# FFN gate and up products of a transformer kernel in another order: pairs of 512-column matmuls, then pairs of 256-column ones

## The chip, the cores and the metric

The kernel runs on one core of a Trainium2 chip. The metric is the device time of one execution in microseconds; the time before is the median of three runs.

## The reference, cut to what matters

Two blocks of two layers each work on 256 tokens with 1024 features. Every layer has two feed-forward networks (FFN), with 2816 hidden features, around its mixers, so eight FFNs are computed in all. The reference in fp32:

```python
D_MODEL, SEQ, DEPTH, D_FF = 1024, 256, 2, 2816

def swiglu(x, w_gate, w_up, w_down):
    return (jax.nn.silu(x @ w_gate) * (x @ w_up)) @ w_down

def first_block(x, ...):
    for l in range(DEPTH):
        x = layer_norm(ALPHA * x + 0.5 * swiglu(x, ffn1_w_gate[l], ffn1_w_up[l], ffn1_w_down[l]), ...)
        ...
        x = layer_norm(ALPHA * x + 0.5 * swiglu(x, ffn2_w_gate[l], ffn2_w_up[l], ffn2_w_down[l]), ...)
    return x
```

The second block has the same form of FFN, with gate and up weights in one matrix. The change touches `x @ w_gate` and `x @ w_up` alone.

## The kernel before

All weights come in pieces of 128x1024 fp32 values (512 KB) through one DMA queue into a ring of six buffers. ScalarE rounds a piece to fp32r, the type of the matmul operands, as `w_hi` (L717); VectorE (in some stages GpSimd) computes the rest, `w_lo = raw - w_hi` (L943). Activations are split likewise; `in_both` holds for each of KD = 8 row tiles k the 256 tokens of the high part and, next to them, the 256 of the low part, and `in_hi` is its first half. A product of full precision is then hi x hi + hi x lo + lo x hi.

For most linear layers the three are three matmuls of 256 columns (`three`, L391 to L393, also used by `begin` for the first gate and up piece of an FFN). For the down product of an FFN and some other outputs they are three matmuls of 512 columns (`three_rows`, L407 to L409).

The gate and up products of the hidden tiles 1 to 21 (`gate_up`) take another form. A piece is the 1024x128 slice of the gate (i = 0) or up (i = 1) weights for a tile of 128 hidden features, as eight row tiles of 128x128. For each row tile k there is one 512-column matmul (L517) with the high weights on both parts of the activations, which goes to the left and right halves of a PSUM bank, and one 256-column matmul (L519) with the low weights on the high part of the activations, which is added to the left half. Each matmul has its own weight load of 128x128 before it. The last matmul of the piece signals `piece_used`; behind that signal ScalarE takes the right half out (L759, `part`) and VectorE adds the left half (L1039), and the split buffer of the piece can be filled again. The engine's program order sets the order of matmuls; for a tile j it is gate piece, up piece, then the down product of tile j - 1 (four banks, twelve matmuls of 512 columns). A gate or up piece begins with a wait for `split_low`, and a down product with waits for its piece and for the hidden values.

Eight FFNs x 21 tiles x 2 pieces x 8 row tiles make 2688 executions of L517 and of L519.

Of the kernel before, what the change touches and what calls it, by code (L numbers as in the profile page):

```python
# [25 lines left out]
S = 256  # L26
LAYERS = 2
KD = D // P
# [116 lines left out]
def build(nc, a, out, stop=None):  # L145
    ctx = ExitStack()
    with ctx:
        def sb(name, shape, dt=F32):
            return ctx.enter_context(nc.sbuf_tensor(name, shape, dt))
# [3 lines left out]
        def sem(name):  # L153

            if name not in sems:
                sems[name] = ctx.enter_context(nc.semaphore(name))
            return sems[name]
# [14 lines left out]
        in_both = sb("in_both", [P, KD, 2, S], F32R)  # L172
        in_hi, in_lo = (in_both[:, :, i, :] for i in range(2))
# [214 lines left out]
        def three(o, left, right, first, last, **kw):  # L388

            (lh, ll), (rh, rl) = left, right  # L390
            nc.tensor.matmul(o, lh, rh, start=first, stop=False, **kw)  # L391
            nc.tensor.matmul(o, lh, rl, start=False, stop=False, **kw)  # L392
            return nc.tensor.matmul(o, ll, rh, start=False, stop=last, **kw)  # L393

        def piece(e, k=KD):

            return [w[:, e % SPLIT, :].rearrange("p (k c) -> p k c", k=k) for w in (w_hi, w_lo)]

        def at2(pair, *index):
            return [v[index] for v in pair]  # L400

        def three_rows(b, e, left_hi, left_lo, first, last, **kw):

            t, d = divmod(b, 2)
            o, tok, cols = ps[:, b, :], slice(t * P, (t + 1) * P), slice(d * 512, (d + 1) * 512)
            right_hi, right_lo = w_hi[:, e % SPLIT, cols], w_lo[:, e % SPLIT, cols]
            nc.tensor.matmul(o, left_hi[:, tok], right_hi, start=first, stop=False, **kw)  # L407
            nc.tensor.matmul(o, left_hi[:, tok], right_lo, start=False, stop=False, **kw)  # L408
            return nc.tensor.matmul(o, left_lo[:, tok], right_hi, start=False, stop=last, **kw)  # L409
# [66 lines left out]
        def gate_up_bank(j, i):  # L476

            return ps[:, 4 + 2 * (j % 2) + i, :]
# [9 lines left out]
        def pe_ffn(pe, n, e0, chunk, seeds=None, fold=None):  # L488


            def begin():


                for c in range(KD // 2):

                    pe.wait_ge(sem("in_ready"), chunk + c + 1)
                    for i in range(TOGETHER):
                        if c == 0:

                            pe.wait_ge(sem("split_low"), e0 + i + 1)  # L500
                        w = piece(e0 + i)
                        for k in (2 * c, 2 * c + 1):
                            mm = three(ps[:, FIRST_BANK, i * S:(i + 1) * S], at2(w, ALL, k, ALL),
                                       at2(given, ALL, k, ALL), k == 0 and i == 0, k == KD - 1, skip_group_check=True)
                        if c == KD // 2 - 1:
                            mm.then_inc(sem("piece_used"), 1)

            def gate_up(j, it=0):
                for i in range(2):
                    e = e0 + 3 * j - 1 + i  # L510

                    pe.wait_ge(sem("split_low"), e + 1 + it * RAW)
                    hi, lo = piece(e)
                    bank = gate_up_bank(j, i)
                    for k in range(KD):

                        nc.tensor.matmul(bank.rearrange("p (a t) -> p a t", a=2), hi[:, k, :], in_both[:, k, :, :], start=(k == 0),  # L517
                                         stop=False, skip_group_check=True)
                        mm = nc.tensor.matmul(bank[:, 0:S], lo[:, k, :], in_hi[:, k, :], start=False, stop=(k == KD - 1),  # L519
                                              skip_group_check=True)  # L520
                    mm.then_inc(sem("piece_used"), 1)

            def down(j, it=0, last=False):
                e = e0 + (FFN_PIECES - 1 if last else 3 * j + 4)
                pe.wait_ge(sem("split_low"), e + 1 + it * RAW)

                pe.wait_ge(sem("hidden_ready"), (ffn0 + n) * TILES + j + 1 + it * 2)
                for b in range(4):
                    if seeds is not None and j == 0 and b % 2 == 0:

                        pe.wait_ge(sem("seeded"), HALF * seeds + b // 2 + 1)
                    mm = three_rows(b, e, hid_hi[:, j % 2, :], hid_lo[:, j % 2, :], j == 0 and seeds is None, last,
                                    skip_group_check=seeds is not None)
                    if last and b < 3:

                        mm.then_inc(sem("rows_out"), 1)
                mm.then_inc(sem("piece_used"), 1)

            def spread():

                pe.wait_ge(sem("diag_ready"), fold + 1)
                for t in range(HALF):
                    mm = nc.tensor.matmul(ps[:, SPREAD_BANK, t * P:(t + 1) * P], ones[:, 0:P], diag[:, t, :], start=(t == 0),
                                          stop=(t == HALF - 1), skip_group_check=True)
                mm.then_inc(sem("spread_ready"), 1)

            begin()
            if fold is not None:
                spread()
            gate_up(1)  # L550
            down(0)
            with pe.Fori(0, TILES // 2 - 1) as it:
                for j in (2, 3):
                    gate_up(j, it)
                    down(j - 1, it)
            down(TILES - 1, last=True)
# [2126 lines left out]
```

## Time and profile before

| | us |
|---|---|
| runs: median (lowest to highest of three) | 2742.33 (2737.32 to 2743.27) |
| profiled execution: span from first to last instruction | 2732.5 |
| TensorE matmuls busy | 2683.6 |
| TensorE weight loads busy (beside the matmuls) | 2350.2 |
| VectorE busy | 1840.9 |
| ScalarE busy | 1401.1 |
| GpSimd busy | 217.3 |

The profile gives the execution by its span alone. Busy time is the time covered by instructions of an engine. Matmuls are pipelined: one starts long before the one ahead of it has ended, so that the rate of TensorE is read from the distances between starts in the timeline, and not from durations. Weight loads overlap the matmul that runs.

### The profile page before, as it was taken

Reading aid. Unit: us, or ns where it says so; the run is one execution under the profiler, and the core shown is the slowest. Engines: PE = TensorE matmul, PEld = TensorE weight load, DVE = VectorE, ACT = ScalarE, POOL = GpSimd, SP = SyncE. Lnnn points to the kernel's source line nnn. Section 1 sums busy time; section 2 is a strip of 40 time slices with the busy share of each in tenths; the row PEclk is TensorE's granted clock in tenths of the full one; section 3 lists DMA queues with packets and bytes.
Section 4 is the critical chain, followed back from the end, with each engine's and each line's share of the span. In section 5 each row is a group of like instructions: output and inputs, shape, how many; then the busy total and the mean of one; then the engine's idle time right before and its main releaser. Section 6 shows DMA issues by size and latency. Waiting matters only on the chain.

```text
span 2732.5 us, 47833 instructions
## 1 busy us (share of the span) xinstructions
PE 2683.6 (98%) x18836; PEld 2350.2 (86%) x18836; DVE 1840.9 (67%) x2891; ACT 1401.1 (51%) x2191; POOL 217.3 (8%) x95
## 2 busy tenths in 40 slices
PE   9999999999999999999999999999999999999999
PEld 7889788888978888889898898888888899998887
DVE  6667766766867677767732856777775863475777
ACT  5455544544564454456623556445446652455544
POOL 0000000000000000005225000000003422400000
PEclk9999999999999999999999999999999999999999
DMA  8765366577535656663413554665674421564564
GB/s 254 216 183 176 105 189 189 174 220 199 167 122 174 188 157 201 187 190 113 116 57 117 174 181 132 196 188 177 185 213 128 123 86 56 162 194 133 177 190 131
DMA packets 623403, 445.38 MB, mean 163 GB/s; under 512 B 28096, under 2 KB 589536, under 8 KB 622880
## 3 DMA queue, kind: packets, MB, share of 16 engines
q1 hardware_dynamic: 623264, 443.43, 54.6%
q8 instruction: 99, 1.62, 0.2%
q14 instruction: 40, 0.33, 0.0%
HBM read 442.32 MB, written 1.05 MB: 162 GB/s over the span
## 4 chain that ended last, share of the span: by engine, by line
PE 89%; DVE 8%; ACT 1%; issue 1%; DMA 0%; POOL 0%; DVEq 0%; SPq 0%; ACTq 0%
PE ps L517 23%; PE ps L519 11%; PE ps L391 8%; PE ps L392 8%; PE ps L393 8%; PE ps L407 7%; PE ps L408 7%; PE ps L409 7%; DVE w_lo L943 2%; PE ps L702 1%; PE ps L678 1%; PE ps L1708 1%; PE ps L1698 1%; PE ps L1670 1%; DVE moments L1111 1%
## 5 line engine op out<-in xcount | busy, mean ns | idle before, releaser
L943 DVE TENSOR_TENSOR w_lo<-raw,w_hi 128x1024 fp32r<-128x1024 f32 x704 | 860.4, 1224 | 418.9 <-ACT w_hi L717 418.1
L717 ACT ACTIVATE w_hi<-raw 128x1024 fp32r<-128x1024 f32 x800 | 844.7, 1056 | 478.6 <-PE ps L409 240.1
L517 PE MATMUL ps<-in_both,w_hi 128*128 128x512 f32 x2688 | 956.4, 398 | 1.7 <-DVE w_lo L943 1.7
L519 PE MATMUL ps<-in_both,w_lo 128*128 128x256 f32 x2688 | 754.1, 281 | 0.0
L517 PEld LDWEIGHTS ps<-in_both,w_hi 128*128 128x128 f32 x2688 | 505.0, 188 | 126.7 <-DVE w_lo L943 4.0
L519 PEld LDWEIGHTS ps<-in_both,w_lo 128*128 128x128 f32 x2688 | 507.5, 189 | 6.1
L391 PE MATMUL ps<-in_both,w_hi 128*128 128x256 f32 x1664 | 486.1, 292 | 23.6 <-DVE in_both L1020 8.3
L392 PE MATMUL ps<-in_both,w_hi 128*128 128x256 f32 x1664 | 471.9, 284 | 0.0
L393 PE MATMUL ps<-in_both,w_lo 128*128 128x256 f32 x1664 | 471.7, 283 | 0.0
L759 ACT ACTIVATE work<-ps 128x256 f32<-128x256 f32 x336 | 129.5, 385 | 538.0 <-PE ps L519 538.0
L943 POOL TENSOR_TENSOR w_lo<-raw,w_hi 128x1024 fp32r<-128x1024 f32 x90 | 216.8, 2413 | 2136.7 <-ACT w_hi L717 2136.7
L391 PEld LDWEIGHTS ps<-in_both,w_hi 128*128 128x128 f32 x1664 | 319.5, 192 | 38.5 <-issue 11.9
L392 PEld LDWEIGHTS ps<-in_both,w_hi 128*128 128x128 f32 x1664 | 319.7, 192 | 1.0 <-issue 0.5
L393 PEld LDWEIGHTS ps<-in_both,w_lo 128*128 128x128 f32 x1664 | 319.7, 192 | 0.0
L407 PE MATMUL ps<-w_hi,hid_hi 128*128 128x512 f32 x704 | 276.9, 393 | 2.4 <-DVE ps L1149 2.4
L408 PE MATMUL ps<-w_lo,hid_hi 128*128 128x512 f32 x704 | 275.9, 392 | 0.0
L409 PE MATMUL ps<-w_hi,hid_lo 128*128 128x512 f32 x704 | 274.1, 389 | 0.0
L1039 DVE TENSOR_TENSOR work<-ps,work 128x256 f32<-128x256 f32 x336 | 141.8, 422 | 105.2 <-ACT work L759 102.7
L407 PEld LDWEIGHTS ps<-w_hi,hid_hi 128*128 128x128 f32 x704 | 132.1, 188 | 36.8 <-DVE ps L1149 3.7
L409 PEld LDWEIGHTS ps<-w_hi,hid_lo 128*128 128x128 f32 x704 | 132.2, 188 | 29.2
L408 PEld LDWEIGHTS ps<-w_lo,hid_hi 128*128 128x128 f32 x704 | 132.2, 188 | 21.0
L991 DVE TENSOR_TENSOR in_both<-arena,in_both 128x512 fp32r<-128x512 f32 x44 | 31.6, 744 | 89.1 <-ACT in_both L723 88.9
(348 smaller groups left out, 3019.7 us busy)
## 6 DMA issues: line engine op xcount, KB each, us to landing
raw<-in_w_ffn_in SPq DMA_DIRECT2D x176, 512.0 KB, 3.7
raw<-in_w_mix SPq DMA_DIRECT2D x112, 512.0 KB, 3.7
raw<-in_ffn_w_gate SPq DMA_DIRECT2D x88, 512.0 KB, 3.8
raw<-in_ffn_w_up SPq DMA_DIRECT2D x88, 512.0 KB, 3.7
raw<-in_ffn_w_down SPq DMA_DIRECT2D x88, 512.0 KB, 3.8
raw<-in_w_ffn_out SPq DMA_DIRECT2D x88, 512.0 KB, 4.0
raw<-in_w_in SPq DMA_DIRECT2D x40, 512.0 KB, 3.8
raw<-in_w_out SPq DMA_DIRECT2D x32, 512.0 KB, 3.5
```

Of the source, the lines that this page charges most:

```text
L391: nc.tensor.matmul(o, lh, rh, start=first, stop=False, **kw)
L392: nc.tensor.matmul(o, lh, rl, start=False, stop=False, **kw)
L393: return nc.tensor.matmul(o, ll, rh, start=False, stop=last, **kw)
L407: nc.tensor.matmul(o, left_hi[:, tok], right_hi, start=first, stop=False, **kw)
L408: nc.tensor.matmul(o, left_hi[:, tok], right_lo, start=False, stop=False, **kw)
L409: return nc.tensor.matmul(o, left_lo[:, tok], right_hi, start=False, stop=last, **kw)
L517: nc.tensor.matmul(bank.rearrange("p (a t) -> p a t", a=2), hi[:, k, :], in_both[:, k, :, :], start=(k == 0), stop=False, skip_group_check ...
L519: mm = nc.tensor.matmul(bank[:, 0:S], lo[:, k, :], in_hi[:, k, :], start=False, stop=(k == KD - 1), skip_group_check=True)
L717: nc.scalar.activation(w_hi[:, e % SPLIT, :], raw[:, e % RAW, :], ACT.Copy).then_inc(sem("split_high"), 1)
L759: nc.scalar.activation(part[:, j % 2, i, :], gate_up_bank(j, i)[:, S:2 * S], ACT.Copy)\
L943: eng.tensor_tensor(w_lo[:, e % SPLIT, :], raw[:, e % RAW, :], w_hi[:, e % SPLIT, :].bitcast(F32), ALU.subtract)\
L1039: nc.vector.tensor_tensor(o, gate_up_bank(j, i)[:, 0:S], part[:, j % 2, i, :], ALU.add).then_inc(sem("summed"), 1)
```

## The change

In `gate_up`, the loop over the eight row tiles becomes a loop over four pairs of neighbouring row tiles. Within a pair the two 512-column matmuls are issued first, and then the two 256-column ones. The same sixteen matmuls with the same operands go to the same bank; the first (k = 0) still starts the accumulation, the last (k = 7, low weights) still ends it and signals the piece. Nothing else is changed.

```diff
-                    for k in range(KD):
-
-                        nc.tensor.matmul(bank.rearrange("p (a t) -> p a t", a=2), hi[:, k, :], in_both[:, k, :, :], start=(k == 0),
-                                         stop=False, skip_group_check=True)
-                        mm = nc.tensor.matmul(bank[:, 0:S], lo[:, k, :], in_hi[:, k, :], start=False, stop=(k == KD - 1),
-                                              skip_group_check=True)
+                    for c in range(KD // 2):
+                        for k in (2 * c, 2 * c + 1):
+
+                            nc.tensor.matmul(bank.rearrange("p (a t) -> p a t", a=2), hi[:, k, :], in_both[:, k, :, :],
+                                             start=(k == 0), stop=False, skip_group_check=True)
+                        for k in (2 * c, 2 * c + 1):
+                            mm = nc.tensor.matmul(bank[:, 0:S], lo[:, k, :], in_hi[:, k, :], start=False, stop=(k == KD - 1),
+                                                  skip_group_check=True)
                     mm.then_inc(sem("piece_used"), 1)
```

## Rows read from the trace of the kernel before

**Rows 1.** The page: busy time, the granted clock in 40 slices, the chain by engine.
```profile
PE 2683.6 (98%) x18836; PEld 2350.2 (86%) x18836; DVE 1840.9 (67%) x2891; ACT 1401.1 (51%) x2191; POOL 217.3 (8%) x95
...
PEclk9999999999999999999999999999999999999999
...
PE 89%; DVE 8%; ACT 1%; issue 1%; DMA 0%; POOL 0%; DVEq 0%; SPq 0%; ACTq 0%
```

**Rows 2.** The page's costliest groups: busy us, mean ns, idle before and its releaser.
```profile
L517 PE MATMUL ps<-in_both,w_hi 128*128 128x512 f32 x2688 | 956.4, 398 | 1.7 <-DVE w_lo L943 1.7
L519 PE MATMUL ps<-in_both,w_lo 128*128 128x256 f32 x2688 | 754.1, 281 | 0.0
```

**Rows 3.** The views of line 517 and line 519: durations in ns, least/median/most.
```profile
L517 PE MATMUL ps<-in_both,w_hi x2688: 389/398/501, 21.0 to 2719.7; 128*128 128x512 f32 x192
...
L519 PE MATMUL ps<-in_both,w_lo x2688: 274/281/284, 21.3 to 2719.9; 128*128 128x256 f32 x192
```

**Rows 4.** Timeline of TensorE, a gate and an up piece: start us, duration us, instruction.
```profile
98.11 0.40 PE L517 MATMUL ps<-in_both,w_hi 128*128 128x512 f32 x1
98.34 0.28 PE L519 MATMUL ps<-in_both,w_lo 128*128 128x256 f32 x1
98.46 0.40 PE L517 MATMUL ps<-in_both,w_hi 128*128 128x512 f32 x1
98.69 0.28 PE L519 MATMUL ps<-in_both,w_lo 128*128 128x256 f32 x1
98.81 0.40 PE L517 MATMUL ps<-in_both,w_hi 128*128 128x512 f32 x1
99.05 0.28 PE L519 MATMUL ps<-in_both,w_lo 128*128 128x256 f32 x1
99.17 0.40 PE L517 MATMUL ps<-in_both,w_hi 128*128 128x512 f32 x1
...
102.35 0.40 PE L517 MATMUL ps<-in_both,w_hi 128*128 128x512 f32 x1
```

**Rows 5.** The same timeline: the last product of the up piece, then the down product.
```profile
102.58 0.28 PE L519 MATMUL ps<-in_both,w_lo 128*128 128x256 f32 x1
102.70 0.40 PE L407 MATMUL ps<-w_hi,hid_hi 128*128 128x512 f32 x1
102.93 0.40 PE L408 MATMUL ps<-w_lo,hid_hi 128*128 128x512 f32 x1
103.17 0.39 PE L409 MATMUL ps<-w_hi,hid_lo 128*128 128x512 f32 x1
...
104.08 0.39 PE L407 MATMUL ps<-w_hi,hid_hi 128*128 128x512 f32 x1
...
105.44 0.39 PE L517 MATMUL ps<-in_both,w_hi 128*128 128x512 f32 x1
```

**Rows 6.** Timeline of TensorE where 512-column products turn into a run of 256-column ones.
```profile
1564.06 0.39 PE L409 MATMUL ps<-w_hi,in_both 128*128 128x512 f32 x1
1564.29 0.28 PE L391 MATMUL ps<-in_both,w_hi 128*128 128x256 f32 x1
1564.40 0.28 PE L392 MATMUL ps<-in_both,w_hi 128*128 128x256 f32 x1
1564.52 0.28 PE L393 MATMUL ps<-in_both,w_lo 128*128 128x256 f32 x1
...
1565.84 0.28 PE L392 MATMUL ps<-in_both,w_hi 128*128 128x256 f32 x1
```

**Rows 7.** Timeline of TensorE where the first FFN's 256-column products end.
```profile
20.92 0.28 PE L393 MATMUL ps<-in_both,w_lo 128*128 128x256 f32 x1
21.04 0.40 PE L517 MATMUL ps<-in_both,w_hi 128*128 128x512 f32 x1
21.28 0.28 PE L519 MATMUL ps<-in_both,w_lo 128*128 128x256 f32 x1
```

**Rows 8.** Busy us (instructions) by engine in one stretch: span, PE, PEld, DVE, ACT, POOL.
```profile
60.00:200.00 140.00, 140.00 (x733) 119.26 (x732) 93.19 (x136) 68.74 (x102) 0.00 (x0) 1.00 0.74 205
```

## Prediction

> **What bounds the kernel now.** I read the page first: TensorE's matmuls are busy for 98% of the span, the granted clock is at its full level in all 40 slices, and the chain that ended last is 89% TensorE [rows 1]. So one nanosecond less on each matmul is one less in the total, and one on any other engine is nothing. The costliest groups come next. L517 and L519, the two lines that the change reorders, hold 956.4 and 754.1 us of the busy time, in 2688 products each, with idle time before L517 of only 1.7 us and before L519 of 0.0 [rows 2]. These stages are then neither waiting for pieces nor for drained banks; what is to be read in them is the distance from one matmul's start to the next. The durations don't give that distance (they overlap), but they tell whether a product was held up: the least duration of L517 is 389 ns and its median 398; L519 has 274 and 281 [rows 3]. The usual product in this loop is about 9 ns (512 columns) or 7 ns (256 columns) longer than the least of its kind.
>
> The distances come from the timeline, whose starts are rounded to 10 ns. I call a 512-column product A and a 256-column product B; "A's distance" is from its start to the next start. In the alternating loop, A takes 0.23, 0.23, 0.24 and B 0.12, 0.12, 0.12, a pattern that repeats in 1.06 us; over twelve pairs, 98.11 to 102.35, it is 4.24 us, so 353.3 ns for a pair [rows 4]. In a long run of A alone the distance is 1.36 us / 6 = 226.7 ns (104.08 to 105.44) [rows 5]. In a long run of B alone it is 1.32 us / 11 = 120.0 ns (1564.52 to 1565.84) [rows 6]. An A and a B from uniform runs would make 346.7 ns; the alternating pair costs 6.7 ns more. That excess, 2688 x 6.7 ns = 18 us, is all that an order can touch if the uniform distances are a floor.
>
> **The change part by part.** No product, operand, column or weight load is added or removed: 2688 A and 2688 B before and after, each with its own load. What moves is the order, from A B A B to A A B B in groups of four; there are 2688 / 2 = 1344 groups. Before, a group costs 2 x 353.3 = 706.7 ns.
>
> The trace of before never shows A A B B in a loop, so I put a group together from the nearest transitions:
> - Two A directly behind a B: at the end of a gate or up piece the last B (102.58) is followed by the down product's A at 102.70, 102.93 and 103.17. The two distances make 0.47 us, against 0.453 for two in a uniform run [rows 5]. The four after these take 0.91 us (103.17 to 104.08), which is 0.227 each, so what a B leaves behind is mostly paid by the first two A [rows 5]. Where A follows a uniform run of B (21.04 to 21.28) the first distance reads 0.24 [rows 7], the same within the rounding.
> - Two B directly behind A: the one place where a run of A turns into a run of B has 1564.29, 1564.40, 1564.52, so 0.23 us for two, against 0.240 in the uniform run [rows 6]. The first B is the quick one (0.11).
>
> The sum of a group: 0.47 + 0.23 = 0.70 us. Each term is good to about 10 ns, which is more than the gain in question, so I choose: 701 ns, because the excess over the uniform 693.3 is then 8 ns for the one change from B back to A in a group, near the 6.7 ns that each such change costs in the alternating loop [rows 4]. The gain is 706.7 - 701 = 5.7 ns a group, and 1344 x 5.7 ns = 7.7 us. The bounds: from below the uniform distances, 2 x 226.7 + 2 x 120.0 = 693.3 ns, a gain of 13.3 ns a group and 18 us [rows 5, 6]; from above the longest single distances that these rows show, 0.24 twice and 0.12 twice, 0.72 us, a loss of 13.3 ns a group and again 18 us, 2760 us [rows 4, 7]; it needs the latest A at both places, and no row has two of 0.24 in a row.
>
> The rest comes to nothing. The last instruction of a piece was a B and is a B, and it carries the same signal, so the engines that wait for a piece are told at the same place; the first A of a piece waits as before. The supply of pieces is covered: in the stretch of 60 to 200 us, all of it gate, up and down, VectorE is busy 93.19 of 140.00 us and ScalarE 68.74, with PE at 140.00 [rows 8]. A piece's gain of 23 ns (four groups) in some 2.8 us is far below the third of that time in which VectorE is idle. The down products start behind B B in place of A B; the transition is the same B to A, and I cost it at nothing.
>
> A rule that speaks against any gain: rows 4 to 6 show that a mixed pair isn't the sum of its uniform distances. The Trainium skill (TensorE: Matmul & The Clock Gate, Back-to-back issue gap) gives the isolated distance as columns over 2.4 GHz plus 2.5 ns, a sum in which the order of products has no part; by it a group costs the same in either order and the time stays. The trace disagrees with its size (120.0 ns for 256 columns is over it) and, by the 6.7 ns, with its being independent of the order.
>
> The result: the median of the three runs is 2742.33 us, the profiled span 2732.5; the 9.8 us between lie outside the first and last instruction or in the spread of runs (2737.32 to 2743.27), and the change doesn't touch them. 2742.3 - 7.7 = 2734.6, so 2735 us. Changes under 0.2% (5.5 us) can't be told from none by measuring this kernel; the forecast is just beyond that.
>
> **The rivals.**
> 1. *The excess belongs to each B, or to nothing that order moves.* The load for the product behind a B has only 0.12 us in which to come in, whatever that product is; if the 6.7 ns are owed for each B wherever it stands, two B owe 13.3 ns and the group stays at 706.7. For it: the first A products of rows 5 show that what a B leaves is paid later, not dropped (0.47 for two). Against it: the uniform run of B owes nothing beyond 120.0 [rows 6]. Time 2742; with what lies between, 2739 to 2744.
> 2. *The excess is gone entirely.* If holding up comes only from A and B taking strict turns, the group costs 693.3 ns and the time is 2742.3 - 18 = 2724 us. For it: both uniform runs are clean [rows 5, 6]. Against: the first two A behind a B are together 17 ns over uniform [rows 5], which the quick first B, 10 ns, doesn't pay back in full.
> 3. *The other side: the hold-ups add.* Two short distances ahead of the A A leave the loads of both late; the two A together cost 0.475, between the 0.47 seen and 0.24 twice, and no B is quick (0.12 each). The place is the pair A A behind B B; the price is 715 - 706.7 = 8.3 ns a group, 1344 x 8.3 ns = 11 us, so 2753 us. It decides as soon as two A directly behind two B cost over 467 ns with B at 120 each. For it: [rows 5] has 0.24 for the second A. Against: [rows 6] has a quick B directly behind A.
>
> That the change doesn't do what it says is no rival here: the order of matmuls on one queue is the program's order.
>
> **How the numbers follow.** The forecast, a group of 699 to 704 ns and 2732 to 2739 us, 0.50. Rival 1, 0.22. Rival 2, 0.13. Rival 3, 0.15. Faster by over 0.2% (below 2736.8): three quarters of the forecast's chance, 0.37, and rival 2, together 0.50. Within 0.2%: the rest of the forecast, 0.13, and nearly all of rival 1, 0.20, together 0.33. Slower by over 0.2%: rival 3 and a little of rival 1, 0.17. The range has to hold most of rival 2 (2724) and a part of rival 3, whose size grows from 0 upward to 2753: 2723 to 2750 us.
>
> **What would show it.** Right: in the timeline of the gate and up stage the starts read about 0.23, 0.24, 0.11 or 0.12, 0.12, a piece of sixteen products takes some 23 ns less than before, and a piece's four groups 2.80 us against 2.83. The median duration of the 512-column line falls from 398 towards 393 ns. Rival 1 shows the same sum of four (0.707) with another split. Rival 2 shows medians at the least durations, 389 for A. Rival 3 shows 0.24 twice and medians of 400 or more. The prediction would be wrong if any idle time before these lines rose above the present 1.7 us by several us, or if the clock row left its level.

## The result, and the profile after

The changed kernel takes 2724.81 us (median of six runs, 2721.28 to 2727.11) against 2742.22 us before (six runs, 2734.24 to 2743.27): a ratio of 0.9946, with a 95% interval of 0.9936 to 0.9956. That is 17.4 us less, or 0.54%. The forecast was 7.7 us less and a time of 2735 us. The direction and the range (2723 to 2750) held; the gain is more than twice the one forecast, and lies beside rival 2 (2724 us) rather than the forecast.

The page of the changed kernel: busy time, the granted clock, the chain by engine, and the two groups that were reordered (now L518 and L521).

```profile
PE 2675.0 (98%) x18836; PEld 2351.4 (86%) x18836; DVE 1835.8 (67%) x2891; ACT 1399.7 (51%) x2191; POOL 216.5 (8%) x95
...
PEclk9999999999999999999999999999999999999999
...
PE 90%; DVE 7%; ACT 1%; issue 1%; DMA 0%; POOL 0%; DVEq 0%; SPq 0%; ACTq 0%
...
L518 PE MATMUL ps<-in_both,w_hi 128*128 128x512 f32 x2688 | 843.6, 395 | 1.9 <-DVE w_lo L945 1.9
...
L521 PE MATMUL ps<-in_both,w_lo 128*128 128x256 f32 x2688 | 528.1, 278 | 0.0
```

Nothing has taken TensorE's place: it is still busy for 98%, and the idle time ahead of the reordered line is 1.9 us, where [rows 2] had 1.7. The busy sums (843.6 and 528.1 us against 956.4 and 754.1) are no measure of the gain, as products that follow one of their own line overlap within a group and are counted once. The mean durations are: 395 ns against 398, and 278 against 281.

The timeline of TensorE around the same tile (start us, duration us, instruction; x2 is two products in a row). It answers to [rows 4] and [rows 5].

```profile
98.05 0.62 PE L518 MATMUL ps<-in_both,w_hi 128*128 128x512 f32 x2
98.52 0.40 PE L521 MATMUL ps<-in_both,w_lo 128*128 128x256 f32 x2
98.75 0.63 PE L518 MATMUL ps<-in_both,w_hi 128*128 128x512 f32 x2
99.22 0.39 PE L521 MATMUL ps<-in_both,w_lo 128*128 128x256 f32 x2
99.45 0.63 PE L518 MATMUL ps<-in_both,w_hi 128*128 128x512 f32 x2
...
102.23 0.40 PE L407 MATMUL ps<-w_hi,hid_hi 128*128 128x512 f32 x1
102.47 0.39 PE L408 MATMUL ps<-w_lo,hid_hi 128*128 128x512 f32 x1
102.70 0.39 PE L409 MATMUL ps<-w_hi,hid_lo 128*128 128x512 f32 x1
102.92 0.39 PE L407 MATMUL ps<-w_hi,hid_hi 128*128 128x512 f32 x1
...
104.96 0.62 PE L518 MATMUL ps<-in_both,w_hi 128*128 128x512 f32 x2
```

From 98.05 to 102.23 there are six groups A A B B: 4.18 us, or 697 ns a group, where two alternating pairs took 706.7 ns. The down product takes 2.73 us (102.23 to 104.96); before it took 2.74 (102.70 to 105.44) [rows 5].

Ten nanoseconds of rounding are coarse for this, so from here on I also give distances (from one product's start to the next start) as medians over the 168 tiles of the FFNs, from the trace's starts in whole nanoseconds. Settled distances are those that repeat once the first products of a piece are past. "Gate" is the piece that stands behind a down product, "up" the one that stands behind the gate piece, "down" the twelve products behind both.

| order in a piece | settled distances, ns | gate | up | down | tile |
|---|---|---|---|---|---|
| A B (before) | 241 120 236 113 233 117 | 2810 | 2830 | 2747 | 8387 |
| A A B B (the change) | 233 236 116 113, 233 231 113 119 | 2777 | 2787 | 2730 | 8294 |

The difference is 93 ns a tile, and 168 x 93 ns = 15.6 us: 12.8 us in gate and up, and 2.9 us in the down products, which the change doesn't touch.

The two profiled spans, 2732.5 and 2725.3 us, differ by only 7.2 us. The missing part is the clock. The view of cores of before, of after, and one stretch of after by engine with the granted clock in the third column from the end:

```profile
core 0: 2732.5 us, clock 0.998
```

```profile
core 0: 2725.3 us, clock 0.995
```

```profile
1310.00:1320.00 10.00, 10.00 (x84) 8.94 (x84) 9.04 (x27) 6.31 (x11) 0.00 (x0) 0.83 0.48 139
```

In a few short stretches, one of them inside this row, the clock is at its lower level (1.2 GHz) although PE counts as busy. The page's clock row, in tenths, doesn't show them; the mean of the core does. The stretch itself, and two of its products:

```profile
1315.20:1318.20 3.00, 3.00 (x14) 3.00 (x15) 2.89 (x7) 0.99 (x2) 0.00 (x0) 0.50 1.05 300
```

```profile
1315.50 0.41 PE L392 MATMUL ps<-w_lo,in_both 128*128 128x256 f32 x1
1315.71 0.41 PE L393 MATMUL ps<-w_hi,in_both 128*128 128x256 f32 x1
```

At this level a 256-column product takes 0.21 us from start to start (213 ns) in place of 120. By the traces' clock records, the clock is low for 6.8 us of before and 23.9 us of after with matmuls running, always in stages other than the gate and up products of tiles 1 to 21; it is low too in the last 1.9 and 4.0 us, where no matmul runs. At 213 ns against 120, 44% of the time at the low level is lost, 3.0 and 10.5 us; if it were half, 3.4 and 11.9 us. Without these, the spans are 2729.5 and 2714.8 us, or 2729.1 and 2713.4: 14.7 to 15.7 us apart, beside the 15.6 us of the tiles. The profiled execution of before was simply one with few such stretches.

### The profile page after: what moved, and what is told of

Read it like the earlier page. It is cut to its first block, busy times and chain, and to the rows that moved or that the text cites. A ratio compares the mean times of both kernels' runs of the same rounds, so it can differ in the third digit from the quotient of the medians.

```text
span 2725.3 us, 47833 instructions
## 1 busy us (share of the span) xinstructions
PE 2675.0 (98%) x18836; PEld 2351.4 (86%) x18836; DVE 1835.8 (67%) x2891; ACT 1399.7 (51%) x2191; POOL 216.5 (8%) x95
## 4 chain that ended last, share of the span: by engine, by line
PE 90%; DVE 7%; ACT 1%; issue 1%; DMA 0%; POOL 0%; DVEq 0%; SPq 0%; ACTq 0%
PE ps L518 22%; PE ps L521 11%; PE ps L391 9%; PE ps L392 8%; PE ps L393 8%; PE ps L407 7%; PE ps L408 7%; PE ps L409 7%; DVE w_lo L945 1%; PE ps L704 1%; PE ps L680 1%; PE ps L1710 1%; PE ps L1700 1%; PE ps L1672 1%; DVE moments L1113 1%
## 5 line engine op out<-in xcount | busy, mean ns | idle before, releaser
L518 PE MATMUL ps<-in_both,w_hi 128*128 128x512 f32 x2688 | 843.6, 395 | 1.9 <-DVE w_lo L945 1.9
L521 PEld LDWEIGHTS ps<-in_both,w_lo 128*128 128x128 f32 x2688 | 504.9, 188 | 117.7
L521 PE MATMUL ps<-in_both,w_lo 128*128 128x256 f32 x2688 | 528.1, 278 | 0.0
L393 PE MATMUL ps<-in_both,w_lo 128*128 128x256 f32 x1664 | 474.5, 285 | 0.0
L518 PEld LDWEIGHTS ps<-in_both,w_hi 128*128 128x128 f32 x2688 | 421.0, 189 | 16.0 <-DVE w_lo L945 3.8
L391 PEld LDWEIGHTS ps<-in_both,w_hi 128*128 128x128 f32 x1664 | 322.6, 194 | 38.7 <-issue 11.7
L392 PEld LDWEIGHTS ps<-in_both,w_hi 128*128 128x128 f32 x1664 | 322.9, 194 | 1.0 <-issue 0.5
```

## The experiments

A is a 512-column product, B a 256-column one, as in the prediction. All kernels are the one before with another body of `gate_up`. Those with halved weights leave out part of the result, and those with 384 columns add something to it that doesn't belong there. These six and the one with the right half of the bank ran once each, so they are read by their distances; their times, in us, follow the tiles to within what the clock makes:

| kernel | time, and before beside it | difference | 168 x difference of a tile |
|---|---|---|---|
| A B, 384 columns | 2879.04, 2738.98 | +140.1 | +141.0 |
| A B, A's weights halved | 2706.55, 2738.98 | -32.4 | -31.4 |
| A B, B's weights halved | 2731.69, 2738.98 | -7.3 | -7.9 |
| A B, right half of the bank | 2737.28, 2738.98 | -1.7 | 0 |
| A B, both halved | 2715.84, 2739.79 | -24.0 | -26.9 |
| A A B B, A's weights halved | 2724.54, 2739.79 | -15.3 | -14.6 |
| A A B B, 384 columns | 2888.29, 2739.79 | +148.5 | +158.9 |

**Longer groups.** The change again, four and four, and eight and eight, all on one chip.

```diff
-                    for c in range(KD // 2):
-                        for k in (2 * c, 2 * c + 1):        # A
-                        for k in (2 * c, 2 * c + 1):        # B
+                    for c in range(KD // n):                # n = 4: quads, n = 8: octs
+                        for k in range(n * c, n * c + n):   # A
+                        for k in range(n * c, n * c + n):   # B
```

> The change itself, beside the two longer groupings. Both theories: 2723 to 2728 us; sixteen products of a piece take 2777 to 2790 ns from start to start in the timeline (before: 2810 to 2830).

> Four 512-column products (A), then their four 256-column ones (B). Theory 'turn': each turn from B back to A costs a fixed few ns over the uniform distances (226.7 for A, 120 for B); the change has one turn in four products and an excess of 3.7 ns over 693.3 there, so one turn in eight halves it: 695.2 ns for four products, a piece of 2781 ns on average, some 2.5 us less in all than the change. Theory 'load': the weight load that runs beside a B is late by about 7 ns wherever B stands; then only the number of B counts, and a piece stays at 2782 to 2790 ns, the time within 1 us of the change.

> All eight A of a piece, then its eight B. Theory 'turn': one turn in sixteen products, a piece at 2773.3 plus about 4 ns = 2777 ns, some 3 to 4 us less than the change. Theory 'load': B distances settle at 120 and A at 226.7, a piece at 2780 to 2790 ns, the time within 1 us of the change.

Measured against 2741.36 us before (eleven runs): the change 2725.15 us, ratio 0.9944 (0.9932 to 0.9956); four and four 2727.24 us, 0.9955 (0.9942 to 0.9967); eight and eight 2723.16 us, 0.9938 (0.9926 to 0.9950). The intervals overlap; the distances are sharper. 'Gate', 'up', 'down' and 'tile' are in ns.

| order in a piece | settled distances, ns | gate | up | down | tile |
|---|---|---|---|---|---|
| A A B B | 233 236 116 113, 233 231 113 119 | 2777 | 2787 | 2730 | 8294 |
| 4 A, 4 B | 235 233 236 224 117 120 120 120, 233 236 228 232 118 119 118 117 | 2780 | 2807 | 2767 | 8354 |
| 8 A, 8 B | 233 236 228 233 231 227 227 227, 113 119 120 ... 120 | 2766 | 2793 | 2748 | 8307 |

The timeline of the kernel with four and four (its up piece and the first product behind it):

```profile
98.41 1.09 PE L517 MATMUL ps<-in_both,w_hi 128*128 128x512 f32 x4
99.33 0.64 PE L519 MATMUL ps<-in_both,w_lo 128*128 128x256 f32 x4
99.81 1.09 PE L517 MATMUL ps<-in_both,w_hi 128*128 128x512 f32 x4
100.74 0.63 PE L519 MATMUL ps<-in_both,w_lo 128*128 128x256 f32 x4
101.21 0.40 PE L407 MATMUL ps<-w_hi,hid_hi 128*128 128x512 f32 x1
```

The timeline of the kernel with eight and eight:

```profile
97.66 1.98 PE L517 MATMUL ps<-in_both,w_hi 128*128 128x512 f32 x8
99.47 1.11 PE L519 MATMUL ps<-in_both,w_lo 128*128 128x256 f32 x8
100.43 2.00 PE L517 MATMUL ps<-in_both,w_hi 128*128 128x512 f32 x8
102.27 1.11 PE L519 MATMUL ps<-in_both,w_lo 128*128 128x256 f32 x8
103.22 0.40 PE L407 MATMUL ps<-w_hi,hid_hi 128*128 128x512 f32 x1
```

The first eight A, behind a down product, take 1.81 us, 226.7 ns each by whole nanoseconds; the second eight, behind eight B, take 1.84 (100.43 to 102.27). The some 27 ns between them are what the first five A pay (233 236 228 233 231). So neither theory holds: the cost of a turn from B to A isn't a fixed few ns (it is 3.7 ns over uniform distances in A A B B, and about 20 in eight and eight), and it isn't the same per B either (four and four is worse than both its neighbours). The forecast of a further 2.5 us for four and four was wrong in sign: by distances it gives back 168 x 60 ns = 10 us. Its median hides this, since its six runs had mean clocks of 0.998 to 1.000, and the before runs beside them 0.993 to 0.998; its profiled execution spans 2724.4 us at a clock of 1.000, with matmuls never at the low level, against 2713.4 to 2714.8 for the change with its low stretches taken off.

**A longer second product.** Alternating, with 384 columns in place of 256.

```diff
-                        mm = nc.tensor.matmul(bank[:, 0:S], lo[:, k, :], in_hi[:, k, :], ...)
+                        mm = nc.tensor.matmul(bank[:, 0:384], lo[:, k, :], in_both[:, k, :, :].rearrange("p a t -> p (a t)")[:, 0:384], ...)
```

> Alternating order of before, but the second product of each row tile has 384 columns in place of 256 (it adds the low weights times 128 more columns, so part of the result is changed). Theory 'load': at 384 columns the load beside it has time enough; no product is held up, every 512-column duration is the least one, 389 ns, and a pair of starts is 226.7 + 170 = 397 ns. Theory 'turn' (unequal lengths cost by themselves): the 512-column durations still vary by 6 to 14 ns and a pair takes about 403 ns.

The timeline, where the starts of the first and the last row are eight pairs apart:

```profile
98.40 0.40 PE L516 MATMUL ps<-in_both,w_hi 128*128 128x512 f32 x1
98.63 0.34 PE L517 MATMUL ps<-in_both,w_lo 128*128 128x384 f32 x1
98.81 0.39 PE L516 MATMUL ps<-in_both,w_hi 128*128 128x512 f32 x1
...
101.65 0.40 PE L407 MATMUL ps<-w_hi,hid_hi 128*128 128x512 f32 x1
```

3.25 us for eight pairs, 407 ns each once settled (distances 233 175 231 175). 'Load' had forecast 397 with every A at its least, 'turn' about 403; both missed. Half as much time again beside a load doesn't make the excess go, so 'load' as it was put on record is out. A B that is longer than the 0.19 us that a whole load lasts as recorded wasn't tried, so that B is too short for the load isn't excluded for every length.

**Half loads.** In the alternating order the weights of one kind of product are cut to 64 columns; the columns moved stay the same.

```diff
-                        nc.tensor.matmul(bank.rearrange(...), hi[:, k, :], in_both[:, k, :, :], ...)
+                        nc.tensor.matmul(bank[0:64].rearrange(...), hi[:, k, 0:64], in_both[:, k, :, :], ...)   # a_half_load, k >= 1
-                        mm = nc.tensor.matmul(bank[:, 0:S], lo[:, k, :], in_hi[:, k, :], ...)
+                        mm = nc.tensor.matmul(bank[0:64, 0:S], lo[:, k, 0:64], in_hi[:, k, :], ...)             # b_half_load, k < 7
```

> Alternating order, but the 512-column product of row tiles 1 to 7 has weights of 64 columns (the upper 64 hidden features get only their first row tile). The load beside each 256-column product is then half as long; columns moved are unchanged. Theory 'load': the excess goes, pairs at 340 ns (226.7 + 113.3), 512-column durations at the least. Theory 'turn': pairs stay at 353 ns.

> Alternating order, but the 256-column product of row tiles 0 to 6 has weights of 64 columns (the upper 64 hidden features lose most of their low weights part). The load beside each 512-column product is half as long, the one beside each 256-column product is whole. Theory 'load': the load that matters is untouched, pairs stay near 353 ns (350 to 354). If what counts is the sum of loading beside streaming, the pair falls to 345 ns or less.

The timeline of the kernel with A's weights halved, loads (PEld) among the products:

```profile
98.17 0.28 PE L517 MATMUL ps<-in_both,w_lo 128*128 128x256 f32 x1
98.17 0.13 PEld L516 LDWEIGHTS ps<-in_both,w_hi 128*64 128x64 f32 x1
98.28 0.39 PE L516 MATMUL ps<-in_both,w_hi 128*64 128x512 f32 x1
98.28 0.19 PEld L517 LDWEIGHTS ps<-in_both,w_lo 128*128 128x128 f32 x1
98.51 0.28 PE L517 MATMUL ps<-in_both,w_lo 128*128 128x256 f32 x1
...
99.30 0.39 PE L516 MATMUL ps<-in_both,w_hi 128*64 128x512 f32 x1
...
99.64 0.39 PE L516 MATMUL ps<-in_both,w_hi 128*64 128x512 f32 x1
```

The load for A starts with the B ahead of it (both at 98.17), and lasts 0.13 us as recorded, where a whole one lasts 0.19. From 98.28 to 99.64 are four pairs in 1.36 us, 340 ns each: 226.7 for A and 113.3 for B, and not one A above 389 ns in the settled part. Halving A's weights alone takes off all of the 13.3 ns by which the alternating pair exceeds 340. What it shortens is the load that runs beside B; but a product with 64 weight columns also writes 64 output rows in place of 128, and no run halves the one without the other, so that the load is what counts is argued and not shown. The timeline with B's weights halved instead (four pairs from the first row to the last):

```profile
100.88 0.39 PE L516 MATMUL ps<-in_both,w_hi 128*128 128x512 f32 x1
101.11 0.28 PE L517 MATMUL ps<-in_both,w_lo 128*64 128x256 f32 x1
101.23 0.39 PE L516 MATMUL ps<-in_both,w_hi 128*128 128x512 f32 x1
...
102.27 0.40 PE L516 MATMUL ps<-in_both,w_hi 128*128 128x512 f32 x1
```

The pair takes about 346.5 ns (229 and 117.5), which lies between the two forecasts (350 to 354, and 345 or less) and meets neither: halving B takes off half of the 13.3 ns as well. Two things follow. First, 120 ns is no floor for B: it is 113.3. The sum from uniform distances that I used as a floor, 693.3 ns a group, is itself held up; the real one, as far as these runs show, is 2 x 340 = 680. Second, the hold-up of the alternating order needs A's weights whole, the ones that are loaded beside the short product.

**Both loads halved.**

> Alternating order; weights of 64 columns in A (row tiles 1 to 7) and in B (row tiles 0 to 6), so the upper 64 hidden features lose most of their sum. Theory 'stretch': a weight load of 128 columns stretches the product beside which it runs by 13.3 ns, one of 64 columns by 6.7 ns (A = 213.3 + load, B = 106.7 + load), and a turn from B to A costs extra only where a whole load runs beside B: a pair takes 220 + 113.3 = 333.3 ns, A 220, B 113.3. Theory 'fixed': each product has 13.3 ns (A) or 6.7 ns (B) of its own, and only the load beside B adds: a pair stays at 340 ns, as with A's weights halved alone.

```profile
100.68 0.39 PE L516 MATMUL ps<-in_both,w_hi 128*64 128x512 f32 x1
100.91 0.27 PE L517 MATMUL ps<-in_both,w_lo 128*64 128x256 f32 x1
...
102.04 0.40 PE L516 MATMUL ps<-in_both,w_hi 128*64 128x512 f32 x1
```

Settled pairs take 340 ns again (227.5 and 112.5; above, four in 1.36 us). 'Fixed' forecast that, and 'stretch' (333.3) is out: halving B's weights on top brings nothing. But the reason that 'fixed' gave, that only the load beside B adds, doesn't fit the run with B's weights halved, which took off 6.8 ns. A's 226.7 ns and B's 113.3 come to 0.443 ns a column for both; that this is what streaming the columns takes is the plain reading, as no run has a faster pair. At 2.4 GHz, a column a cycle would be 0.417.

**The other half of the bank.** B adds to the right half of the bank.

```diff
-                        mm = nc.tensor.matmul(bank[:, 0:S], lo[:, k, :], in_hi[:, k, :], ...)
+                        mm = nc.tensor.matmul(bank[:, S:2 * S], lo[:, k, :], in_hi[:, k, :], ...)
```

> Alternating order, but the 256-column product is added to the right half of the bank, not the left (the result keeps its value in sum, since both halves are added later). The next 512-column product then begins at columns that were not written last. Theories 'load' and 'turn': unchanged, 353.3 ns a pair. A third theory, that A waits for B's additions to the same PSUM columns: the pair falls to 340 to 347 ns.

Every median distance is the same as before to the nanosecond (241 120 236 113 233 117). The product's mean duration in the groups is the same 398 ns as in [rows 2]:

```profile
L516 PE MATMUL ps<-in_both,w_hi 128*128 128x512 f32 x2688 | 956.4, 398 | 1.7 <-DVE w_lo L940 1.7
```

Which half of the bank B adds to has no part in it.

**The change with half loads, and with 384 columns.** Both in the order A A B B, with the edits shown above.

> The order of the change (A A B B) with 64-column weights in A of row tiles 1 to 7. Theory 'stretch': each of A A B B is stretched by the load beside it: 220 (beside the second A's half load), 226.7, 120 (beside the second B's whole load), 113.3: 680 ns a group, and no turn cost as the load beside the last B is a half one. Theory 'fixed': 226.7, 226.7, 120 then 113.3, 686.7 ns.

> The order of the change with 384 columns in the second kind of product (part of the result is changed as in the alternating run with 384). 'Stretch' gives 2 x 226.7 + 2 x 173.3 = 800 ns a group over uniform distances; the alternating run took 814 (2 x 407). If the turn is what costs, one turn in a group leaves 800 + 7 = 807; if pairs are a lucky case for 256 columns alone, it stays at 814.

With A's weights halved, the group A A B B didn't settle at 680 or 686.7 ns: the gate piece takes 2753 ns (688 a group) and the up piece 2798 ns (about 700), so the up piece is worse than with whole loads (2787), and no pattern repeats in it (229 231 117 120, 235 230 117 117, 233 236 112 116, 233 234 117 121). With 384 columns, the settled group takes 827 ns (237 233 180 176), against 814 for two alternating pairs and 807 forecast:

```profile
99.07 0.64 PE L517 MATMUL ps<-in_both,w_hi 128*128 128x512 f32 x2
99.54 0.52 PE L519 MATMUL ps<-in_both,w_lo 128*128 128x384 f32 x2
99.90 0.64 PE L517 MATMUL ps<-in_both,w_hi 128*128 128x512 f32 x2
```

All that the expectations of these two runs forecast is missed. Pairs are better than alternation for 512 and 256 columns (697 against 706.7) and worse for 512 and 384 (827 against 814). That grouping gains isn't a rule.

**Groups of three, and eight with pairs.**

```diff
+                    for ks in ((0, 1, 2), (3, 4, 5), (6, 7)):   # triples: A for all of ks, then B
+                    w = 8 if i == 0 else 2                      # oct_pair: eight in the gate piece, pairs in the up piece
```

> Groups A A A B B B twice and A A B B once in a piece, three turns in place of four. The turn costs measured so far are 6.7 ns (A B), 3.7 (A A B B), 14 to 18 (four and four), 20 (eight and eight): a turn costs more the longer the run of A behind it, up to what five A pay. From the row of the first three A behind a B (233, 236, 228, less 680) a turn is 17 less what quick B give back (7): 10 ns twice and 4 once, a piece of 2773.3 + 24 = 2797 ns, some 3 us more than the change in all at the same clock. If the turn cost were fixed at 3.7, a piece would take 2784.

> The gate piece (which comes behind a down product, a long run of A) takes eight A and then eight B, the up piece pairs as in the change. If the distances depend on the few products just ahead and can be put together from the runs so far, the gate piece takes 2766 ns (as with eight and eight), the up piece 2787 (as in the change), the down product behind it 2730 (as in the change): 8283 ns for a tile against 8294 in the change and 8387 before, 168 x 11 ns = 1.9 us less than the change at the same clock, too little for the medians to show. If they can't be put together, the up piece behind a long run of B comes out at 2800 ns or more and nothing is gained on the change.

Groups of three: 2727.16 us against 2739.79, ratio 0.9950 (0.9937 to 0.9964). The up piece takes 2798 ns, one more than was put together from rows for it (2797), and the tile 2786 + 2798 + 2730 = 8314 ns. Eight with pairs: 2726.20 us against 2736.81, ratio 0.9962 (0.9948 to 0.9975). Gate 2766 and up 2787 ns came out to the nanosecond; the down product behind it took 2747 and not 2730, so the tile takes 8300 ns, no better than the change (8294). The reason is to be seen in the distances: this up piece ends in 114 119 where that of the change ends in 116 113, and the A behind them pay for it, in whole nanoseconds 233 236 228 233 231 here and 233 231 227 227 227 there (in the timeline 2.74 us for the twelve here, 101.90 to 104.64, and 2.73 there):

```profile
101.67 0.40 PE L520 MATMUL ps<-in_both,w_lo 128*128 128x256 f32 x2
101.90 0.40 PE L407 MATMUL ps<-w_hi,hid_hi 128*128 128x512 f32 x1
...
102.59 0.40 PE L407 MATMUL ps<-w_hi,hid_hi 128*128 128x512 f32 x1
...
104.64 1.98 PE L518 MATMUL ps<-in_both,w_hi 128*128 128x512 f32 x8
```

No order that was tried is measurably faster than the change; eight and eight is as fast by the medians (0.9938 and 0.9944, with intervals that overlap). By the distances it is 168 x 13 ns = 2.2 us behind; five of its six runs had mean clocks of 0.997 or 0.998, those of the change 0.995 to 0.997.

## Why the prediction was right or wrong

*What bounds the kernel*: right. TensorE stayed the bound, nothing took its place, and the idle time before the lines rose by 0.2 us.

*The group*: right in its way, wrong in size. Taken from transitions it came to 0.70 us, I took 701 ns, and the settled groups take 698 and 696 by turns. In a difference of 5.7 ns, being 4 ns off is most of it: 1344 x 4 ns = 5.4 us. The parts show where. The two transitions taken from before, 0.47 and 0.23 us, are 469 and 232 ns in whole nanoseconds, together the 701. In one kind of group the two A take just that, 469, and the two B are quicker, 116 and 113 = 229 ns; in the other the two B take 232 and the two A are quicker, 464. No row of before showed either. So an up piece takes 2.79 us where the signs had 2.80, and the median duration of the 512-column line is 395 ns where they had 393. And every gate piece starts with a group behind a long run of A, 227 227 113 119 = 686 ns, which I left out of the sum. It adds no gain: before starts that piece as cheaply (227 113 233 117 = 690), so the gate piece falls by 33 ns and the up piece by 43.

*"The transition is the same B to A, and I cost it at nothing"*: wrong. This is the step that failed. The down product fell from 2747 to 2730 ns, since the A behind the last B start 233 231 227 and no longer 233 236 228 233 231; 168 x 17 ns = 2.9 us. I had in hand that what B leaves is carried over into the products behind it [rows 5], and didn't apply it to the products that the change itself doesn't move. I had also read it as too short: from the rounded 0.91 us I took 0.227 for each of the four A behind the first two, where whole nanoseconds have 228 233 231 227. What B leaves is paid by five A and comes to some 27 ns, not by two and to 17.

With these, 7.7 + 5.4 + 2.9 = 16.0 us, near the 15.6 us of the tiles and inside the interval of the ratio (12.1 to 17.6 us).

*The bounds*: the lower one was no bound. It took uniform distances for a floor, and the half loads showed that uniform B products are held up themselves (120 against 113.3 ns). Rival 2, "the excess is gone entirely", gave the right time for the wrong reason: the groups are still above uniform (697 against 693.3), and its 18 us are matched only with the down product's help. The measured time lies in the range because the range was drawn to take in rival 2, and that was in part luck. Rivals 1 and 3 are out: the group fell by 9.7 ns, and B is quick behind A A. A loss by pairing, as rival 3 had it, does come about where 384 columns are paired (827 against 814); whether by the ground that I gave, late loads, no run shows.

*The 9.8 us between the span and the median of the runs*: only 1.8 us of it lie outside the first and last instruction (2727.11 us for the span of 2725.3); the rest goes with the clock: the profiled execution had a mean of 0.998, and of 30 other runs of this kernel, beside the experiments, 24 had 0.993 to 0.997. The clocks of the three runs behind the 2742.33 aren't on record. I named the spread of the runs as one of two places, and didn't look at the mean clock, which tells it.

*The rule of the Trainium skill*: the Trainium skill (TensorE: Matmul & The Clock Gate, Back-to-back issue gap) gives the order of products no part in the isolated distance. The runs disagree: five orders of the same sixteen products took 2787 to 2830 ns in the up piece. The Trainium skill (the same title, Step-by-step: what each phase is for) says that loading the next weights takes no SBUF read bandwidth from the running product. The half loads don't tell whether it is bandwidth, but with A's weights halved the A behind B fell from between 233 and 241 ns to 226.7.

What stays open is the state that is carried along. The runs show that it depends on the width of A's weights, and less on that of B's, in the alternating order, that it takes two A to clear it behind the change, five behind before and behind eight and eight, and nine behind four and four (the down product there starts 235 233 236 224 231 236 228 232 231), that it isn't the half of the bank, and that the same group can cost 686, 696 or 698 ns by what stands ahead. They don't show what it is: neither a fixed price for a turn nor one for each load fits alternation, pairs, fours, eights and the 384-column runs together. Two things weren't varied at all: the length of a load apart from the rows that its product writes, and which activations stand next to each other (in A B A B a B reads the same columns as the A ahead of it, in A A B B no B does). That the change's order is good here is measured, and not explained.

## What to carry to other kernels

Where TensorE is busy throughout, read the distances between starts in a uniform run and in the mixed one; if the mixed one is above their sum, the order is worth a try, but try it with the sizes at hand, since the pairs that won 10 ns with 256 columns lost 13 with 384. Count the neighbours too: up to ten products behind the short ones were still off their uniform distance here, so an edit also changes stages that it doesn't touch. For changes under 1%, compare spans with the mean granted clock beside them, and trust distances before medians.

## What the runs showed of the hardware

- fp32r products stream at 0.443 ns a column (226.7 ns for 512, 113.3 for 256) at the full clock in the fastest pairs seen, each with its own weights, those of the 512-column products halved; a uniform run of 256-column products with whole loads takes 120.0, and 213 at the low clock level.
- A 512-column product varies from 224 to 241 ns in its distance by the products ahead of it, in patterns that repeat to within a nanosecond or two in nearly all of the 168 tiles (before and after; the 224 is from four and four).
- Halving the stationary columns of the 512-column products alone took 13.3 ns off each alternating pair, although not one moving column was saved; halving those of the 256-column products alone took 6.8 ns, and halving both no more than 13.3.
- The clock goes to its lower level for a few short stretches while PE counts as 100% busy, at places and in numbers that differ by kernel and run; in the traces here, never among the gate and up products of tiles 1 to 21. Mean clocks of 0.993 to 0.999 go with differences of over 12 us between runs of one kernel (before: 2733.46 us at 0.999, 2746.08 us at 0.993).
